# Attention layers in pairs of heads inside the projections, and no GpSimd arithmetic there: a 12-layer FP32 transformer stack on Trainium2

## The reference

```python
# stick: causal, weights from a reversed cumulative sum
z = einsum('bqhd,bshd->bhqs', q, k)
between = cumsum(log_1m, reverse=True) - log_1m
att = where(earlier, exp(log_sigmoid(z) + between), 0)
# dsa: every query keeps its 64 best keys of an index score (8 index heads), then softmax
q, k = rope(rms_norm(q, q_norm)), rope(rms_norm(k, k_norm))
score = einsum('bqh,bqhs->bqs', wi, relu(qi . ki));  top_k(score, 64)
# multi: 4 heads with a position bias, 6 with dilated windows (partial rotation),
# 6 with shared keys (axial rotation); every q and k head normed; outputs normed by family
mix = concat([rms_norm(out_a), rms_norm(out_d), rms_norm(out_c)]);  x + mix @ w_out
```

## Time and profile before

| | |
|---|---|
| median of 3 runs | 2528.54 us (2527.0 to 2528.85) |
| the profiled execution | 2532.53 us; its span 2530.8 us |
| mean granted TensorE clock | 0.954 |
| PE busy | 2361.4 us, 93% of the span |
| DVE busy | 1579.6 us, 62% |
| ACT busy | 1192.0 us, 47% |
| POOL busy | 174.2 us, 7% |
| PE's share of the chain that ended last | 80% (DVE 11%, ACT 5%, issue 2%, POOL 1%) |

### The profile page before, as it was taken

One profiled execution on the slowest core, in us unless ns is written; L12 is line 12 of the kernel. 1 busy time (PEld: TensorE's weight loads), 2 busy tenths in 40 slices (PEclk: granted clock), 3 DMA queues, 4 the chain that ended last, 5 costly groups with the idle time before them and its releaser, 6 DMA issues.

```text
span 2530.8 us, 55813 instructions
## 1 busy us (share of the span) xinstructions
PE 2361.4 (93%) x22886; PEld 2207.9 (87%) x22886; DVE 1579.6 (62%) x2350; ACT 1192.0 (47%) x1988; POOL 174.2 (7%) x249
## 2 busy tenths in 40 slices
PE   6799899998999998999987998999999999998999
PEld 5689799998899997599976897999986999977998
DVE  6744365665665666666577543655666777766776
ACT  5533444435544462654455333544556444556443
POOL 1000010010100111010010000100210000211000
PEclk8889999999999998899988899999999999999999
DMA  4220155542455341165522201555422554423553
GB/s 170 92 85 4 44 189 193 177 139 75 136 188 197 129 154 63 42 202 180 191 75 92 84 4 44 183 196 177 142 92 80 190 179 166 150 67 110 187 177 125
DMA packets 88434, 327.16 MB, mean 129 GB/s; under 512 B 9808, under 2 KB 9936, under 8 KB 87632
## 3 DMA queue, kind: packets, MB, share of 16 engines
q1 hardware_dynamic: 87984, 322.72, 38.4%
q0 software_dynamic: 288, 2.10, 0.2%
HBM read 323.73 MB, written 1.05 MB: 128 GB/s over the span
## 4 chain that ended last, share of the span: by engine, by line
PE 80%; DVE 11%; ACT 5%; issue 2%; POOL 1%; DMA 0%; DVEq 0%; ACTq 0%; SPq 0%; POOLq 0%
PE bank L1220 16%; PE bank L1221 16%; PE bank L1222 16%; PE bank L1242 4%; PE bank L1243 4%; PE bank L1244 4%; DVE w_split L1784 3%; ACT w_split L1514 2%; PE bank L491 2%; PE bank L1410 2%; PE bank L500 1%; DVE h_split L1812 1%; PE bank L1389 1%; PE bank L514 1%; PE bank L1400 1%
## 5 line engine op out<-in xcount | busy, mean ns | idle before, releaser
L1220 PE MATMUL bank<-h_split,w_split 128*128 128x256 f32 x3168 | 920.6, 291 | 36.4 <-DVE h_split L1812 22.8
L1221 PE MATMUL bank<-h_split,w_split 128*128 128x256 f32 x3168 | 905.3, 286 | 0.0
L1222 PE MATMUL bank<-h_split,w_split 128*128 128x256 f32 x3168 | 904.1, 285 | 0.0
L1784 DVE TENSOR_TENSOR w_split<-ring_a,w_split 128x1024 fp32r<-128x1024 f32 x468 | 569.1, 1242 | 208.6 <-ACT w_split L1514 207.2
L1220 PEld LDWEIGHTS bank<-h_split,w_split 128*128 128x128 f32 x3168 | 611.5, 193 | 52.9 <-DVE h_split L1812 32.5
L1221 PEld LDWEIGHTS bank<-h_split,w_split 128*128 128x128 f32 x3168 | 606.6, 191 | 2.1
L1222 PEld LDWEIGHTS bank<-h_split,w_split 128*128 128x128 f32 x3168 | 606.1, 191 | 0.0
L1514 ACT ACTIVATE w_split<-ring_a 128x1024 fp32r<-128x1024 f32 x468 | 476.8, 1049 | 133.8 <-PE bank L1222 122.1
L1242 PE MATMUL bank<-act_split,d_split 128*128 128x256 f32 x1008 | 285.1, 283 | 2.4 <-DVE act_last L1861 2.4
L1243 PE MATMUL bank<-act_split,d_split 128*128 128x256 f32 x1008 | 285.1, 283 | 0.0
L1244 PE MATMUL bank<-act_split,d_split 128*128 128x256 f32 x1008 | 285.0, 283 | 0.0
(11 more groups left out here) (277 smaller groups left out, 3300.5 us busy)
## 6 DMA issues: line engine op xcount, KB each, us to landing
ring_a<-wa SPq DMA_DIRECT2D x474, 512.0 KB, 4.4
ring_d<-wd SPq DMA_DIRECT2D x132, 512.0 KB, 4.4
tab_sb<-tab SPq DMA_DIRECT2D x1, 2448.0 KB, 13.3
planes<-na POOLq DMA_DIRECT2D x2, 1024.0 KB, 6.5
xT<-x SPq DMA_DIRECT2D x1, 1024.0 KB, 4.8
out<-xT SPq DMA_DIRECT2D x1, 1024.0 KB, 3.9
vec_sb<-vec SPq DMA_DIRECT2D x1, 288.0 KB, 4.9
tab_sb<-tab SPq DMA_DIRECT2D x1, 65.0 KB, 4.6
```

The source lines that it names most:

```text
L1220: mm(dst, w[:, 0, ks], x[:, 0, k, :], start=(k == 0), stop=False)
L1221: mm(dst, w[:, 0, ks], x[:, 1, k, :], start=False, stop=False)
L1222: last = mm(dst, w[:, 1, ks], x[:, 0, k, :], start=False, stop=(k == KT - 1))
L1784: v.tensor_tensor(w_split[:, u % 4, 1, :], ring_a[:, u % 4, :], w_split[:, u % 4, 0, :].bitcast(f32), ALU.subtract).then_inc(s["w_lo"], 1)
```

## The change

In the three attention kinds the weights are laid out by pairs of heads, so that three consecutive units give q, k and v of one pair (in dsa after 6 index units), and each engine's program becomes one loop over "slots", one unit each, with a pair's attention steps at fixed distances behind its units. `FIRST` is the number of units ahead of the pairs, `LAG` how many slots the attention steps stand back further, `OUT_SLOTS` where the eight output units stand after the last projection. `pair_at(L, n, d)` gives the pair t whose step of distance d falls into slot n, that is n = FIRST + 3t + d.

```diff
+FIRST = {"stick": 0, "dsa": 6, "multi": 0}
+LAG = {"stick": 0, "dsa": 6, "multi": 0}
+OUT_SLOTS = {"stick": (0, 1, 2, 3, 4, 5, 6, 7), "dsa": (0, 1, 2, 3, 4, 7, 10, 12),
+             "multi": (0, 1, 2, 3, 4, 5, 6, 7)}
+PAIR_ORDER = (2, 3, 4, 5, 6, 7, 0, 1)
...
+        def att_pe(pe, L, unit, norm):
...
+            for n in range(N + OUT_SLOTS[kind][-1] + 1):
+                if n < N:
+                    one(n)
+                elif n - N in OUT_SLOTS[kind]:
+                    out_unit(OUT_SLOTS[kind].index(n - N))
...
+                t = pair_at(L, n, 8 + lag)
+                if t is not None:
+                    pv(t)
+                t = pair_at(L, n, 7 + lag)
+                if t is not None:
+                    turn(t, 1)
+                t = pair_at(L, n, 6 + lag)
+                if t is not None:
+                    turn(t, 0)
...
+                t = pair_at(L, n, 4 + lag)
+                if t is not None:
+                    scores(t)
+                t = pair_at(L, n, 3)
+                if t is not None:
+                    turn_v(t)
+                t = pair_at(L, n, 2)
+                if t is not None:
+                    norm_rope(2 * t + 1)
+                t = pair_at(L, n, 1)
+                if t is not None:
+                    norm_rope(2 * t)
...
+        def att_act(act, L, A, hi, root, step, inverse_root):
...
+                t = pair_at(L, n, 3)
+                if t is not None:
+                    norm_rope_root(2 * t + 1)
+                t = pair_at(L, n, 2)
+                if t is not None:
+                    norm_rope_root(2 * t)
+                    norm_rope_in(2 * t + 1)
...
+                if n + AHEAD < N + KT:
+                    hi(L, n + AHEAD)
...
+                t = pair_at(L, n, 5 + lag)
+                if t is not None:
+                    exps(t)
...
+        def att_dve(dve, L, v, step, lo, rms_inverse, add_banks):
...
+                    step.did(v.tensor_tensor(x, x, T("cos" + rope), ALU.mult))
...
+                t = pair_at(L, n, 3)
+                if t is not None:
+                    norm_rope(2 * t + 1)
+                t = pair_at(L, n, 2)
+                if t is not None:
+                    norm_rope(2 * t)
+                t = pair_at(L, n, 5 + lag)
+                if t is not None:
+                    shifted(t)
+                if 0 < n < N + KT - AHEAD:
+                    lo(L, n + AHEAD)
+                t = pair_at(L, n, 6 + lag)
+                if t is not None:
+                    normed(2 * t)
+                    normed(2 * t + 1)
...
-                            nc.gpsimd.tensor_tensor(x, x, T("cos" + rope), ALU.mult).then_inc(s["cos_ready"], 1)
```

More of the change, by code:

```diff
@@ L83, in repeat, with rope_of @@
         self.n, self.off = before + count * per, 0
[L86 to L106, removed]
+FIRST = {"stick": 0, "dsa": 6, "multi": 0}
+LAG = {"stick": 0, "dsa": 6, "multi": 0}
+GAIN_OF = {"stick": 0, "dsa": 0, "multi": 1}
+OUT_SLOTS = {"stick": (0, 1, 2, 3, 4, 5, 6, 7), "dsa": (0, 1, 2, 3, 4, 7, 10, 12), "multi": (0, 1, 2, 3, 4, 5, 6, 7)}
+PAIR_ORDER = (2, 3, 4, 5, 6, 7, 0, 1)
+def rope_of(kind, t):
+    return "0" if kind == "dsa" else ("1", "1", "1", "2", "2", "2", None, None)[t]
 def plan_layers(layers):
@@ L118, in plan_layers @@
                         convs=sum(o["kind"] == "ffn" and o["idx"] >= 4 for o in out),
+                        outs=sum(o["kind"] not in ("ffn", "rwkv") for o in out),
                         multis=sum(o["kind"] == "multi" for o in out)))
@@ L1139, in rwkv_pool, with unit_bank, norm_rope_bank, squared @@
                 g_.tensor_scalar(sq[:, k, 0:1], hT[:, k, 0:1], -1.0, None, ALU.mult).then_inc(s["xx_ready"], 1)
+        OUT_BANKS = {"multi": (4, 2, 5, 7), "dsa": (4, 2, 5, 7), "stick": (4, 7, 0, 5)}
+        def unit_bank(s):
+            return B[4 + s % 3]
+        def norm_rope_bank(L, n):
+            return B[(7, 2)[(n + (L["kind"] == "dsa")) % 2 == 0]]
+        def squared(i):
+            return extra[:, i % 4, :]
+        def gained_(i):
+            return extra[:, 4 + i % 4, :]
+        def root_(i):
+            return work[:, i % 4, :]
@@ L1497, in _ @@
                     pe.wait_ge(s["tab_loaded"], 16)
-                dict(ffn=ffn, stick=stick, dsa=dsa, multi=multi,
-                     rwkv=lambda L: rwkv_pe(pe, L, product, out_proj))[L["kind"]](L)
+                if L["kind"] == "ffn":
+                    ffn(L)
+                elif L["kind"] == "rwkv":
+                    rwkv_pe(pe, L, product, out_proj)
+                else:
+                    att_pe(pe, L, unit, norm)
         @block.scalar
@@ L1544, in norm @@
                 else:
+                    if not after_mixer:
+                        for b in range(4):
+                            squares(b)
                     root_table()
@@ L1548, in norm, with squares @@
                         hi(L, n)
+            def squares(b):
+                x2, q2 = [t[:, 2 * b:2 * b + 2, :].rearrange("p a b -> p (a b)") for t in (xT, sq)]
+                A(q2, x2, ACT.Square).then_inc(s["squared"], 1)
             def root(L):
@@ L1947, in projections @@
-            def projections(L):
-                count = PROJ[L["kind"]]
-                for n in range(count):
-                    if n + AHEAD < count:
-                        lo(L, n + AHEAD)
-                    if n == 0:
-                        rms_inverse(L)
-                    if not (L["kind"] == "dsa" and n == 21):
-                        evac_scaled(L, n, row_of(L["kind"], n))
-                    for t in tiles_after(L["kind"], n):
-                        norm_rope(L, t, row_of(L["kind"], t), t < 16, rope_of(L["kind"], t))
@@ L2264, in blocks, with in_pairs @@
     return w.reshape(KT, P, n, P).transpose(2, 1, 0, 3).reshape(n, P, KT * P)
+def in_pairs(b, order=range(KT)):
+    return np.stack([b[[t, KT + t, 2 * KT + t]] for t in order]).reshape(3 * KT, P, D)
 def padded(w, n):
```

1158 lines of the change are left out of this document (568 added, 590 removed).

## The result

The changed kernel takes 2585.78 us (median of 4 runs, 2583.6 to 2587.88), the kernel before beside it 2528.69 us. The ratio is 1.0226, 95% interval 1.0208 to 1.0244: slower by 2.3%.

A forecast was written before the change was run, and what follows sets the result against it. PE bounded the kernel before; afterwards the order of waits would bound multi and dsa. 2532.5 + 11 (layers and seams) + 22 (clock) = 2565.5, less 4.0 to the median: 2562 us, range 2500 to 2605.

The forecast's parts named there:

- the second form of rival 4: In the attention loops, the ring's PE work runs cold for 3.5 us a period: 2606 us, chance 0.1.
- The ring: Multi and dsa loops: waits through PE, ACT and DVE give 18.8 us a rotated pair, PE idle 5 before `turn(t, 0)`.
- Rival 2: Attention loops: engines overlap and PE bounds at 13.8 us a pair, 2456 us; shorter ring 2480 to 2523; chance 0.22.
- The clock: Behind the ring's 5 us idles, 19 in all, half clock costs 1.75 us in two of three: 22 us.
- the first form of rival 4: The ring runs at half clock throughout, PE's 27.6 us becoming the period: about 2700 us, chance 0.03.
- dsa: Dsa layer: first ring about 88 us in, five periods 93, tail 37.7, sum 219 against 214.1: +5, -10 to +15.
- multi: Two multi layers: 182 us each against 170.7 and 172.4, so +11 and +10, -3 to +20 each.
- stick: Stick layer: no ring, PE's work sums to 135 us, so -14; bounds -20 and -5.
- rival 3: In stick a pair's steps wait for each other, the layer stays at 149 us: total 2576, chance 0.07.
- Seams: At ten layer-to-layer seams: the rest counted as 0, between -1 and +1 each; less 1 us in the sum.
- Cosine: Cosine product on DVE: two tiles a pair, 0.43 us each, lying in the ring; POOL's part vanishes.
- Scores: Attention scores: four matmuls of 64 rows, 0.97 us to the next start; PE wins 1.7 to 2.6 us a pair.

The follow-up runs named there:

- Runs 1 to 4: Changed kernel reordered: normalising first on DVE, 2527.07 us; `shifted` first, 2532.62; both, 2489.55; both plus ACT's copy of the first turned weights first, 2474.59.
- run 5: Changed kernel with 7 extra matmuls (0.43 us each), later overwritten, ahead of the wait of each `turn(t, 0)`: 2565.21 us.
- run 4: Changed kernel with normalising and `shifted` moved earlier on DVE, and ACT's copy of the first head's turned weights at its slot's start: 2474.59 us.
- run 7: Changed kernel with normalising and `shifted` moved earlier, plus the old GpSimd rms norm of x in ten layers: 2519.96 us against 2489.55 without that norm.
- Run 8: Kernel with both DVE orders changed and ACT's copy first (2474.6 us), its scores' matmuls over all 128 rows instead of 64: 2488.05 us.
- run 2: Changed kernel with `shifted` (scale, bias, maximum) ahead of the even tile's norm on DVE instead of behind it: 2532.62 us.

## Why the prediction was right, and where it was not

The prediction had the direction, and the time lies in its range; but the change of +33.5 us was measured as +57.1, and 2585.8 is 1 us beyond the bounds of the forecast itself (2545 to 2585), towards the second form of rival 4 (2606). Of the miss of 24 us, 15 lie in dsa and 6 in the two multi layers; stick gives 5 back; the seams have 4, and the step from the profiled execution to the median another 4 (2585.33 and 2585.78 for the changed kernel, where I took 4.0 off). So the mechanism was right, and the total comes from a large error in dsa and smaller ones on both sides. Step by step:

- **The ring** was read rightly out of the orders: S to turn 12.3 us (1861.1 to 1873.43) for 12.7, idle 4.17 for 5, and the rest 8.2 with the half clock where 6.1 at full clock was said (S is the start of the unit behind the even norm on PE). Runs 1 to 4 show it as the cause: with three changes of order alone, and the same work, 111 us go, and PE's 13.8 us become the period. Rival 2, that PE bounds the loops from the start, falls by the same runs; it became true only once they were reordered.
- **The clock** was right in kind and too small. I put 1.75 us on two of three periods, 22 us in all; the filled idle shows 2.2 in each. In the first multi layer the turns behind 5.38, 4.16, 4.17, 4.18, 4.18 and 3.20 us of idle have records of 1.00 to 1.12 us, those behind 1.25 and 0.92 have 0.66. Such idles stand ahead of 16 turns (6, 6 and 4 in dsa) instead of the 19 of the sum, and all 16 bring the half clock, in dsa sometimes only behind the turn; by an estimate from run 5 that is up to 16 x 2.2 = 35 us. The Trainium skill, "TensorE: Matmul & The Clock Gate", section "Loop structure matters more than you think", says that long waits between matmuls send PE cold, and the trace agrees; but only the work just behind the idle was at half clock, in multi the turn and 10 to 21 matmuls of a unit, so the first form of rival 4 did not come.
- **dsa is the step that failed in size**: +5 (and some 6 of clock) was forecast, +26.0 measured. My sum was 88 + 93 + 37.7, measured are 94.6 + 102.4 + 43.8 = 240.8. First, top-k was to lie beside the projections, with the ring's first unit at 88 us; it was at 94.6, and without top-k the layer is 11 us shorter, so DVE bounds those slots. Second, the five periods: four of 20.0 to 20.4 us against 18.6, and a fifth of 21.7, in which PE waits 6.76 us ahead of an output unit (1035.09). Third, the end: the spread-out output units don't fill the softmax chain of the last pairs, PE waits 3.68 us ahead of two turns (1061.90 and 1075.33), and 22 and 12 matmuls behind them are at half clock. This last part is read in the trace, and no run took it apart; run 4 still has both waits.
- **multi**: +11 and +10, with the clock some +19 and +18 by the prediction's own terms, against +22.0 and +21.4. In the first of them unit 5 starts after 25.7 us (27 said), the seven periods, with most of the output norm's sums, take 139.4 (127.6 said, without the clock) and the tail 28.3 (27.4 said).
- **stick**: -14 forecast, -19.3 measured. PE is busy for 128.4 of 130 us there, so no wait of a pair took the idle's place and rival 3 falls. The sum of the terms, 135, is 4.5 us above the measured layer: the entry took 10.4 us to unit 2 (531.29) instead of 12, which is 1.6 of it. The rest, about 3, is in the block: its products, counted whole at 35.9 us, are now split by rows and columns, and no run took that apart.
- **Seams**: -1 forecast, +2.7 in all from the table (rwkv and ffn rows). That hides larger things on both sides. Behind multi and dsa the ffn is 2.4 us longer; in the trace PE waits 1.45 us there for DVE, behind dsa for the first low part (1088.91), behind multi for the first product of the ffn (2005.74, 2398.31), and the norm's 8 matmuls take 3.3 us to the next start. Behind stick the same norm stands without this wait, and the ffn is 1.9 us shorter; before, 19 of its matmuls were at half clock behind the norm. No run took these apart. GpSimd's norm in this structure costs 30 us more (run 7): I had priced the low parts at 0.47 against 1.04 and missed that PE's first units wait for all eight.
- **Cosine**: in the ring, as said, but 0.47 us a period instead of 0.9.
- **Scores**: 0.97 us from the index row was right (1.07, with full rows 1.73, and 13.5 us in all). "TensorEngine Tiling (Array Packing)", section "Key Properties", of the Trainium skill says that a switch of mode drains TensorE. Run 8 shows what two of the four switches of a pair cost, about 0.2 us together; for all four that makes 0.4 (an estimate), the bound that I named and did not count.

## What to carry to other kernels

When work of two stages is interleaved slot by slot, follow one item round all the engines' orders and add up what stands ahead of each wait: if that ring is longer than any engine's sum, the shares of busy time don't show it (here 91, 60 and 47%). Here 4.3% of the whole program lay in the order of three groups of instructions, none of which changed its cost. An idle in such a ring costs twice when the clock falls behind it; filling it with matmuls that nobody reads then won 20.6 us, and taking it away by the order 111.

## What the runs showed of the hardware

- In the multi layers of the changed kernel the TensorE clock was at half behind every idle of 3.2 to 5.4 us, for the turn or a part of it and 10 to 21 matmuls of the unit, and at full behind those of 1.25 us or less. Between these the length of one idle did not decide: 2.32 us behind the norm of x left it full in the first multi layer (1807.38) and brought it to half in the second (2198.80); in run 2, 1.84 and 1.83 us brought the half clock and another 1.83 did not; in run 4, 3.18 us (1012.62) did not. With the idle cut from 4.17 to 3.70 us, 21 matmuls were at half clock instead of 16, so a shorter idle is no proof of a gain.
- The clock also fell with no idle ahead. In dsa one unit has 48 products of 8 columns (L1179 to L1181) instead of 24 of 256; while they run, with PE busy all the time, the clock falls to half (871.4), and it is full again at 881.6. From 871.5 to 876.9 PE is busy for all of 5.4 us at a granted clock of 0.50. What brought it down there no run tested.
- VectorE's low parts took 1.0 us each beside GpSimd's squares and 0.43 without; the kernel with these squares was 3 us a layer slower on the mean, though PE had 6 matmuls less.
- Four products of 64 rows on alternate halves of the array took 1.07 us, of 128 rows 1.73; the two switches around them cost about 0.2 us.
